# When GpSimd writes the residual stream after a LayerNorm: in a kernel of six transformer layers on one Trainium2 core

## The reference

```python
for i in range(4):                     # first block
    y = mixer(i, x)                    # 0: sliding attention, 1: gated recurrence, 2: latent attention, 3: sliding
    x = layer_norm(ALPHA * x + y, ln_g[i, 0], ln_b[i, 0])
    x = layer_norm(ALPHA * x + memory_cross_attention(x, mem_k, mem_v, x_w_q[i], x_w_o[i]), ln_g[i, 1], ln_b[i, 1])
    x = layer_norm(ALPHA * x + conv_glu_ffn(x, f_w_up[i], f_conv_w[i], f_conv_b[i], f_w_down[i]), ln_g[i, 2], ln_b[i, 2])
for l in range(2):                     # second block: h is the residual stream
    h = h + attention_heads(rmsnorm(h, norm_mix[l]), rmsnorm(mem, norm_mem[l])) @ w_out[l]
    h = h + conv_ffn(rmsnorm(h, norm_ffn[l]), w_up[l], conv_w[l], conv_b[l], w_down[l])
return rmsnorm(h, norm_final)
```

## Time and the profile before

| | |
|---|---|
| median of 3 runs | 2376.48 (2375.91 to 2378.72) |
| the profiled execution, its own time | 2377.84 |
| its span, first to last instruction | 2376.5 |
| mean granted TensorE clock | 0.945 |
| busy: PE, DVE, ACT, POOL | 2130.2 (90%), 1615.2 (68%), 1217.9 (51%), 180.3 (8%) |
| chain that ended last, by engine | PE 77%, DVE 12%, ACT 5%, issue 4%, POOL 1%, DMA 1% |

### The profile page before, as it was taken

The page is one execution under the profiler, slowest core; times in us unless marked ns, Lnnn a source line. Parts: engine busy times, 40 slices in busy tenths (PEclk is TensorE's granted clock), DMA queues, the critical chain, the costliest instruction groups (busy, mean ns, idle before and its releaser), DMA issues.

```text
span 2376.5 us, 34303 instructions
## 1 busy us (share of the span) xinstructions
PE 2130.2 (90%) x13752; PEld 1932.7 (81%) x13752; DVE 1615.2 (68%) x2639; ACT 1217.9 (51%) x2105; POOL 180.3 (8%) x165
## 2 busy tenths in 40 slices
PE   8878899897899979889988787999788999888998
PEld 7757799796789978779987576998777999767997
DVE  4665777787577777577777656776565776766776
ACT  4444455483365555345545444554544655555554
POOL 3001200202010020220001012000000000000000
PEclk9998999898999989899998998999898999999999
DMA  9313566454366643346643134665422766423662
GB/s 286 123 54 113 157 195 185 122 166 140 111 184 187 178 130 124 124 128 200 186 161 128 54 129 144 188 186 151 138 81 86 209 186 185 136 89 116 199 187 94
DMA packets 435454, 352.90 MB, mean 148 GB/s; under 512 B 15869, under 2 KB 381750, under 8 KB 435296
## 3 DMA queue, kind: packets, MB, share of 16 engines
q1 hardware_dynamic: 429296, 332.49, 46.3%
q0 software_dynamic: 6000, 18.22, 2.2%
HBM read 349.62 MB, written 1.05 MB: 148 GB/s over the span
## 4 chain that ended last, share of the span: by engine, by line
PE 77%; DVE 12%; ACT 5%; issue 4%; POOL 1%; DMA 1%; ACTq 0%; SPq 0%; DVEq 0%; POOLq 0%
PE psum L497 19%; PE psum L498 18%; PE psum L499 18%; PE psum L909 14%; PE psum L815 2%; PE psum L802 2%; DVE xt_lo L1453 2%; DVE w_lo L1438 1%; DVE stat L1729 1%; DVE n_tok L1816 1%; PE psum L772 1%; DVE e L1724 1%; ACT xt_hi L1087 1%; POOL norm L2013 1%; ACT w_hi L1027 1%
## 5 line engine op out<-in xcount | busy, mean ns | idle before, releaser
L1438 DVE TENSOR_TENSOR w_lo<-w_raw,w_hi 128x1024 fp32r<-128x1024 f32 x639 | 751.4, 1224 | 193.8 <-ACT w_hi L1027 193.1
L497 PE MATMUL psum<-xt_hi,w_hi 128*128 128x256 f32 x2744 | 794.5, 290 | 70.2 <-ACT xt_hi L1087 50.3
L498 PE MATMUL psum<-xt_lo,w_hi 128*128 128x256 f32 x2744 | 791.7, 289 | 0.0
L499 PE MATMUL psum<-xt_hi,w_lo 128*128 128x256 f32 x2744 | 790.9, 288 | 0.0
L1027 ACT CAST w_hi<-w_raw 128x1024 fp32r<-128x1024 f32 x639 | 645.1, 1047 | 97.0 <-PE psum L499 71.9
L497 PEld LDWEIGHTS psum<-xt_hi,w_hi 128*128 128x128 f32 x2744 | 542.6, 198 | 81.0 <-ACT xt_hi L1087 54.5
L498 PEld LDWEIGHTS psum<-xt_lo,w_hi 128*128 128x128 f32 x2744 | 542.6, 198 | 4.4
L499 PEld LDWEIGHTS psum<-xt_hi,w_lo 128*128 128x128 f32 x2744 | 542.1, 198 | 0.0
L1892 DVE SCALAR_TENSOR_TENSOR qt<-psum,par,qt 128x255 f32<-128x255 f32 (+1 forms) x528 | 218.1, 476 | 152.1 <-ACT qt L1355 151.8
L497 PE MATMUL psum<-w_hi,xt_hi 128*128 128x512 f32 (+4 forms) x700 | 255.9, 366 | 20.5 <-ACT xt_hi L1087 11.6
L498 PE MATMUL psum<-w_lo,xt_hi 128*128 128x512 f32 (+4 forms) x700 | 253.3, 362 | 0.0
(11 more groups left out here) (223 smaller groups left out, 2197.5 us busy)
## 6 DMA issues: line engine op xcount, KB each, us to landing
w_raw<-in_f_w_up_dram SPq DMA_DIRECT2D x176, 512.0 KB, 5.1
w_raw<-in_f_w_down_dram SPq DMA_DIRECT2D x88, 512.0 KB, 5.0
w_raw<-in_w_up_dram SPq DMA_DIRECT2D x88, 512.0 KB, 4.9
w_raw<-in_w_down_dram SPq DMA_DIRECT2D x44, 512.0 KB, 5.1
w_raw<-in_x_w_q_dram SPq DMA_DIRECT2D x32, 512.0 KB, 4.6
w_raw<-in_x_w_o_dram SPq DMA_DIRECT2D x32, 512.0 KB, 4.9
w_raw<-in_a_w_qkv_dram SPq DMA_DIRECT2D x24, 512.0 KB, 4.6
w_raw<-in_w_in_fox_dram SPq DMA_DIRECT2D x20, 512.0 KB, 4.9
```

The costliest lines, as they stand in the source:

```text
L497: self.eng.matmul(out, stat[0], mov[0], start=first, stop=False)
L498: self.eng.matmul(out, stat[0], mov[1], start=False, stop=False)
L499: return self.eng.matmul(out, stat[1], mov[0], start=False, stop=last)
L1438: self.up(self.eng.tensor_tensor(self.m.lo[:, s, :], self.m.raw[:, s, :], self.m.hi[:, s, :].bitcast(F32), ALU.subtract), "w_lo", u)
```

## The change

GpSimd waits, ahead of its passes, until VectorE has written the last low part of the operand of the next stage (`ready` of feature tile KT - 1 = 7). It stands in `norm_finish` of class `Pool`, so it acts at eleven LayerNorms: all of the first block except the last, which has its own code on VectorE.

```diff
     def norm_finish(self, l, k):
         m = self.m
         self.wait_ge("rows_in", self.tag)
+
+        self.wait_ge("ready", (self.tag, "norm"), KT - 1)
         for b in range(TB):
             x = m.x_tok[:, b, :]
             self.wait_ge("normed", self.tag, "norm", b)
```

## The result

| | before | after |
|---|---|---|
| median, four runs each, us | 2376.3 (2375.91 to 2378.72) | 2398.6 (2396.8 to 2399.96) |
| span of the profiled execution, us | 2376.5 | 2398.1 |
| mean granted clock of TensorE over the span | 0.945 | 0.944 |

The ratio is 1.0091 with a 95% interval of 1.0074 to 1.0109: the change makes the kernel slower by 22.3 us, 0.9%. The forecast was 2392.5, in a range of 2376 to 2402, with 0.78 on slower.

The account below looks back on a forecast made before the run. TensorE, busy nine tenths of the span, was read by its waits, largest at stage entries. Waits summing to +8.0 and cold clock restarts of +8.0 took 2376.5 to 2392.5, with an 8-in-10 range of 2376 to 2402.

Parts of the forecast that it names:

- The entry: Start of a stage: L1816 at 0.8 instead of 2.82, all L1453 near 0.7; the four cross stages sum to -13.6.
- The turn-taking: After an entry, GpSimd passes and VectorE's four weight splits alternate, one split per 3.3, ending 13.4 after the last L1453.
- T: End of the last L1453 of a stage's entry, for which GpSimd now waits; forecast 4.9 earlier at ffn0.
- Rival (2): VectorE keeps the port while it has splits queued, passes fill gaps; faster, 2363; chance 0.1.
- rival (3): GpSimd reaches its first pass only after one or two splits; gains and late loads cancel, 2376 to 2381; chance 0.1.
- ffn0 to ffn2: Feed-forward stages: convolution L1892 behind held splits makes TensorE wait at tile 2; +3.0 together, +9.0 with the clock.
- Rival (1): Delays as computed, but clock stays up or mix1's short operations slip through; 2384.5 down to 2377; chance 0.2.
- the cover argument: At ffn0, TensorE reached tile 2 2.9 after the convolution was done; held splits use up this cover, and TensorE waits 4.5.
- ffn3: Load of mem_2 queued on GpSimd behind the passes, which end 8.0 later, all on the path; +8.0, already cold.
- mix3: Load of the sinks queued behind passes delays copy L1542 and splits; TensorE waits 8; +4.2, or +6.2 with clock.
- mix2: Factor of the latent norm, on GpSimd behind the passes and loads, comes later, so L1652 starts later; +3.0, no clock cost.
- mix1: Four short lambda operations (L1633, L1635, L1636, L1637) each run into a pass, shifting what follows; +3.4, no clock cost.

Follow-up runs that it names:

- e1: Changed kernel with the wait kept only at the four entries of cross stages; 2365.76 us, ratio 0.9952 to the kernel before.
- e3: Changed kernel with each pair of GpSimd passes replaced by six memsets of x_tok, which read nothing; 2370.26 us, ratio 0.9973 to the kernel before.
- e5: Changed kernel with 18 zero products filling TensorE's wait ahead of tile 2 in ffn0 to ffn2; 2391.04 us, ratio 1.0059 to the kernel before.
- e4: Changed kernel with VectorE's first convolution of each feed-forward stage after two low splits, not four; 2387.21 us, ratio 1.0045 to the kernel before.
- e9: Changed kernel with 36 zero products ahead of TensorE's third convolution tile in mix1; 2396.69 us, ratio 1.0076 to the kernel before.
- e7: Kernel before, plus the wait at cross entries and ffn0 to ffn2's passes spread over tiles 4, 6, 8, 10; 2353.72 us, ratio 0.9899.
- e6: Changed kernel with the load of mem_2 issued ahead of GpSimd's passes at the entry of ffn3; 2387.81 us, ratio 1.0044 to the kernel before.
- e2: Changed kernel with the wait kept only at the entries of ffn0 to ffn2; 2387.02 us, ratio 1.0043 to the kernel before.

## Why the prediction was right, and where a term was off

**The entry, right.** L1816 was forecast at 0.8 and measured at 0.81, L1453 at 0.7 and 0.69. The cross stages gave 13.8 for 13.6, and e1, which has only these, 13.7.

**The turn-taking, right.** One event carried the forecast that VectorE and GpSimd alternate, with the fourth split ending 13.4 after T. It ended 13.6 after T (275.03 less 261.42). GpSimd started 0.14 after T and not 0.07, still 0.12 ahead of VectorE. Rival (2), in which VectorE keeps the port, falls with the 13.35 of the splits, and rival (3), in which GpSimd reaches its first pass too late to hurt, with 261.56. e3 shows that the holding is by what the passes read.

**ffn0 to ffn2, right in both halves.** The wait for L1892 was forecast at 4.5 in ffn0 and was 5.05. Of the +9.1, the filled wait of e5 gives 5.4 back (5.2 to 6.3 by the other profiles), near the 6.0 for the clock; the remaining 3.7 stands against 3.0. Rival (1), clock up, is out by the 0.50 of the windows. e4 confirms the cover argument: with the convolution only two splits deep the stages are back at about the time of before.

**ffn3, right.** The first product behind the splits comes 18.68 later on the time line, less 10.82 by which the stage was entered late: 7.9, for 8.0. The rest of the 9.1 is the clock. I took ffn3 as cold already and so as no dearer, but in this profile the half-rate stretch behind the restart, 3.3 before, lasts until 1490:

```profile
1489.00:1490.00 1.00, 1.00 (x7) 0.50 1.07 313
```

That is 6.0, 2.7 more at half rate, which cost 1.35. It isn't a cost of the change that always comes: in e5 and e9, whose ffn3 is the same code, the stretch behind this restart lasts 3.4 and 3.5, and the stage loses 7.95 and 7.98, the 8.0 of the forecast. TensorE in e9, where it restarted at 1483.36:

```profile
1486.00:1487.00 1.00, 1.00 (x7) 0.57 1.10 217
```

**mix3, right.** The copy of the sinks, VectorE:

```profile
1276.28 0.18 DVE L1542 COPY qrt<-small 128x32 f32<-128x32 f32 x1 [14.52 <-DMA small<-in_a_sinks_dram]
```

It is 15.79 later than in the earlier trace rows, less 7.46 on entering: 8.3, as forecast. TensorE waited 7.78 for the split, 8 in the forecast, and the stage lost 6.8 (up to 7.8 in other profiles) for 6.2.

**mix2, right.** L1652 starts at 885.16, 9.05 later than in the earlier trace rows, less 5.70 on entering: 3.35 for 3.0. No experiment moves this one by itself, so here the cause rests on the time line; the stage lost 3.2 to 4.5 in five profiles.

**mix1, the term that was off: +5.3 for +3.4.** The chain of lambda on VectorE, with the second and the last of GpSimd's passes:

```profile
470.52 1.71 DVE L1633 TENSOR_SCALAR small<-small 128x8 f32<-128x8 f32 x1 [0.75 <-ACT small L1146]
472.27 0.20 DVE L1634 RECIPROCAL small<-small 128x8 f32<-128x8 f32 x1
472.28 2.40 POOL L2047 TENSOR_TENSOR x_tok<-x_tok,bias_row 128x1024 f32<-128x1024 f32 x1
472.50 2.20 DVE L1635 TENSOR_TENSOR small<-small 128x8 f32<-128x8 f32 x1
474.74 2.27 DVE L1636 TENSOR_TENSOR small<-small 128x8 f32<-128x8 f32 x1
477.05 0.17 DVE L1637 TENSOR_SCALAR small<-small 128x8 f32<-128x8 f32 x1
477.07 2.35 POOL L2047 TENSOR_TENSOR x_tok<-x_tok,bias_row 128x1024 f32<-128x1024 f32 x1
477.25 3.19 DVE L1639 SCALAR_TENSOR_TENSOR small<-small 128x8 f32<-128x8 f32 x6
...
490.27 1.52 DVE L1582 SCALAR_TENSOR_TENSOR kt<-psum,par,kt 128x255 f32<-128x255 f32 x3 [0.77 <-ACT kt L1152]
```

Undisturbed, one of these takes 0.17 (L1637) and the six of L1639 took 1.17 in the kernel before. So four short instructions are held, as forecast (L1633, 1.71, L1635, L1636 and one of L1639), though the fourth is not L1637. TensorE restarts 2.59 later than in the earlier trace rows and entered the stage 0.52 earlier: 3.1 for 3.4. The step that failed is the clause "In mix1 and mix2 VectorE is behind anyway", by which I gave mix1 no clock cost. A restart at half rate follows the wait of 8.92, TensorE then delivers late to ScalarE and this to VectorE, and VectorE is not behind: L1582 waits 0.77 in the last line above. e9 measures that term by itself, 2.4 at L1593, against the 0 in the forecast. With the 3.1 of the delay that makes 5.5, where L1593 came 5.6 later and the stage ended at +5.27.

**What is left.** Of the 5.5 between the sums (6.1 between the forecast and the median), mix1 has 1.9, ffn3 1.1, mix3 0.6 and the second block 1.6. Of these only the part of mix1, and perhaps mix3's, comes back in most of the other profiles. The second block is untouched. A window of TensorE shows where its 1.6 lies; it starts 14 ahead of the block and ends 18 ahead of its last norm:

```profile
1667.29:2370.65 703.36, 651.65 (x4293) 0.95 0.48 144
```

The same stretch of the program in the kernel before runs from 1647.39 to 2349.11, 701.72 long, and as many products kept TensorE busy there for 647.47 at a clock of 0.96. So it is 4.2 more of busy time for the same work, at a lower granted clock, and 2.5 less of waiting. Why the half-rate stretches were longer there isn't shown; in the untouched second blocks of e1 to e7 and e9 the difference lies between 0.0 and 1.5.

## What to carry to other kernels

Work that collides with VectorE for the port doesn't go away when it is moved out of a serial stretch: price it where it lands, split by split, and ask which queued instruction behind the held ones is wanted first. Where four passes in a row have to be absorbed, spread them over a stretch in which VectorE has slack, and put each load or factor that shares GpSimd's queue ahead of them. A new wait of TensorE long enough for the granted clock to fall costs its restart as well, also in a stage where another engine seems to set the pace.

## What the hardware showed that I had not expected

The holding has no smallest size here: instructions of 128x8, which take 0.17 undisturbed, took 1.71 to 2.27 in mix1, and L1647 with 128x2 took 1.10 in e6. Whether one is held went by which of the two started first. L1633, L1635 and L1636 started while a pass was running, and each ended within 0.03 of its end (472.23, 474.70 and 477.01, the passes at 472.21, 474.68 and 476.98). The two that passed between them started just ahead of a pass, L1634 at 472.27 (pass at 472.28) and L1637 at 477.05 (pass at 477.07). L1634 is a RECIPROCAL, but L1637 is of the same kind as the held L1633, so nothing here says that RECIPROCAL is exempt.

L1892 reads PSUM and one SBUF operand of 128x255, and is not held: in e4 its four took 1.64 from 267.81 on, inside the pass that ran from 266.76 to 270.16, and 1.66 before. Its 1.64 in the changed kernel shows nothing, since the last pass was over at 273.95.

The price of a cold restart varies more than I had allowed, and the length of the wait doesn't fix it. After a wait of 4.87 in ffn2 TensorE ran at half rate for 2.8 in the changed kernel, and after one of 4.95 at the same place in e2 for 6.1; in ffn3 it was 6.0 in the changed kernel and 3.4 and 3.5 in e5 and e9. At half of that each, a restart costs 1.4 to 3.0. Zero products in the wait kept the granted clock at 1.00 and gave 1.2 to 2.4 back.
